# A fused two-layer backbone: three of five adaptive rounds summed on VectorE, and the zero stores moved behind the 22nd group

## The reference

```
s_lat = jax.nn.silu(c)
s_ctx = jax.nn.silu(c_ctx)
for layer in range(DEPTH):
    mod_l = jnp.split((s_lat @ ada_w[layer] + ada_b[layer])[:, None, :], 6, axis=-1)
    mod_c = jnp.split((s_ctx @ ada_w[layer] + ada_b[layer])[None, None, :], 6, axis=-1)
    hl = modulate(rmsnorm(xl, norm_g[layer, 0]), mod_l[0], mod_l[1])
    hc = modulate(rmsnorm(xc, norm_g[layer, 0]), mod_c[0], mod_c[1])
    ... mixer (layer 0: retention and a gated linear recurrence; layer 1: attention), then
    ... a mixture of 32 experts, top 2 of a group, for every token
return rmsnorm(xl, final_norm_g)
```

## Time and profile before

| | before |
|---|---|
| median of 3 runs | 2051.31 us (2050.94 to 2054.58) |
| the profiled execution | 2053.72 us |
| its span, first to last instruction | 2052.0 us |
| mean granted TensorE clock in it | 0.914 |
| TensorE matmul busy in the span | 1720.2 us (84%) |
| VectorE busy | 679.7 us (33%) |
| ScalarE busy | 439.6 us (21%) |
| GpSimd busy | 272.4 us (13%) |
| groups of this stage on TensorE | from 40.30 us to 350.67 us |

### The profile page before, as it was taken

One profiled execution on the slowest core, in us unless ns is written; L12 is line 12 of the kernel. 1 busy time (PEld: TensorE's weight loads), 2 busy tenths in 40 slices (PEclk: granted clock), 3 DMA queues, 4 the chain that ended last, 5 costly groups with the idle time before them and its releaser, 6 DMA issues. The chain is left out here.

```text
span 2052.0 us, 26634 instructions
## 1 busy us (share of the span) xinstructions
PE 1720.2 (84%) x9184; PEld 875.8 (43%) x9185; DVE 679.7 (33%) x1211; ACT 439.6 (21%) x842; POOL 272.4 (13%) x393
## 2 busy tenths in 40 slices
PE   5999999899899789996629999999977799765560
PEld 2443344645445334443317455555543344332230
DVE  3404765743312111111134337774332111111114
ACT  3104453211011101111124135553101101111012
POOL 1002440311101000001022220000111001000001
PEclk9999999998899899998868999999979899877775
DMA  9887744443599999999962002002379999999984
GB/s 371 272 296 235 268 160 144 168 157 140 216 358 406 418 411 417 416 417 410 425 244 90 39 7 87 1 1 96 142 278 399 411 416 414 412 415 421 420 359 149
DMA packets 99608, 559.64 MB, mean 273 GB/s; under 512 B 17188, under 2 KB 37376, under 8 KB 59976
## 3 DMA queue, kind: packets, MB, share of 16 engines
q1 hardware_dynamic: 86288, 521.34, 64.0%
q0 software_dynamic: 7744, 20.98, 3.0%
q10 hardware_dynamic: 5496, 16.26, 2.1%
HBM read 522.88 MB, written 40.91 MB: 275 GB/s over the span
## 5 line engine op out<-in xcount | busy, mean ns | idle before, releaser
L2198 PE MATMUL exp_gps<-moew_wg,all_hT 128*32 128x256 f32 x832 | 128.4, 477 | 102.9 <-DMA moew_wu<-in_moe_w_up 95.3
L577 PE MATMUL abp_ps<-home_pieces,all_hT 128*128 128x512 f32 x384 | 169.8, 597 | 0.6 <-PE abp_ps L581 0.3
L2204 PE MATMUL exp_gps<-moew_wg,all_hT 128*64 128x512 f32 (+1 forms) x272 | 137.8, 642 | 28.7 <-DMA moew_wu<-in_moe_w_up 24.3
L2353 DVE TENSOR_TENSOR all_hT<-all_hT,exp_ups 64x512 f32<-64x512 f32 (+1 forms) x30 | 20.7, 690 | 369.3 <-ACT all_hT L2289 369.3
L2205 PE MATMUL exp_ups<-moew_wu,all_hT 128*64 128x512 f32 (+1 forms) x272 | 136.6, 638 | 0.0
L2198 PE MATMUL exp_ups<-moew_wu,all_hT 128*32 128x256 f32 x832 | 128.3, 477 | 0.0
L2204 PE MATMUL exp_gps<-home_pieces,all_hT 128*128 128x512 f32 (+1 forms) x208 | 108.8, 635 | 22.2 <-DMA home_pieces<-in_moe_w_up 20.9
L2198 PEld LDWEIGHTS exp_gps<-moew_wg,all_hT 128*32 128x32 f32 x832 | 56.8, 136 | 160.4 <-issue 142.0
L577 PEld LDWEIGHTS abp_ps<-home_pieces,all_hT 128*128 128x128 f32 x384 | 71.4, 190 | 99.1 <-issue 97.5
L2351 DVE TENSOR_TENSOR all_hT<-all_hT,exp_ups 64x256 f32<-64x256 f32 x34 | 14.4, 425 | 283.6 <-ACT all_hT L2287 283.6
L2205 PE MATMUL exp_ups<-home_pieces,all_hT 128*128 128x512 f32 (+1 forms) x208 | 107.8, 630 | 0.0
(11 more groups left out here) (457 smaller groups left out, 2986.1 us busy)
## 6 DMA issues: line engine op xcount, KB each, us to landing
moew_wg<-in_moe_w_gate SPq DMA_DIRECT2D x43, 2048.0 KB, 25.0
moew_wu<-in_moe_w_up SPq DMA_DIRECT2D x43, 2048.0 KB, 31.7
moew_wd<-in_moe_w_down SPq DMA_DIRECT2D x43, 2048.0 KB, 39.6
home_pieces<-in_moe_w_gate SPq DMA_DIRECT2D x21, 2048.0 KB
home_pieces<-in_moe_w_up SPq DMA_DIRECT2D x21, 2048.0 KB
home_pieces<-in_moe_w_down SPq DMA_DIRECT2D x21, 2048.0 KB
all_X<-in_ada_w SPq DMA_DIRECT2D x40, 1024.0 KB, 8.3
ys<-abp_zero SPq DMA_DIRECT2D x32, 448.0 KB, 8.8
```

The costliest lines, as they stand in the source:

```text
L577: last = nc.tensor.matmul(ps[i % RB][:], hT[:, kk, what * P:(what + 1) * P], w[n % S][:, kk, :], start=(kk == 0), stop=(kk == KD - 1))
L2198: last = nc.tensor.matmul(bank[lo + j * Q:lo + (j + 1) * Q, 0:HC], x[:, k, 0:Q], wt[:, k, j * HC:(j + 1) * HC], start=(k == 0), stop=(k == ...
L2204: nc.tensor.matmul(gps[0:rows, :], x[:, k, 0:rows], w.g[q][:, k, :], start=(k == 0), stop=(k == KD - 1))
L2353: nc.vector.tensor_tensor(h[at:at + rows, :], sg[at:at + rows, :], ups[at:at + rows, :], ALU.mult).then_inc(h_done, 1)
```

## The change

Rounds 2 and 3 stay on TensorE, one step behind each of groups 2 to 9 and 26 to 33, with a ring of two buffers. Rounds 1, 4 and 5 are summed by VectorE: for each chunk `ada_sum` multiplies the 128 x 2048 chunk by the column of `sT` that belongs to it and adds it into a sum of 128 x 2048 that stays spread over the partitions. Round 1 has two sums (latent and context), rounds 4 and 5 one (latent). The chunks come through four buffers of their own. When a round's eight chunks are in, TensorE adds over the partitions (`reduce`), with a stationary operand `pick` that has a column of ones, behind group 15 (8 matmuls), 18 and 21 (4 each). The order of the rounds' outputs becomes 2, 1, 4, 5, 3. All 43 zero stores stand behind group 21 in SyncE's program, three for each group's turn.

```diff
-        RING = 3
+        TURNED = (2, 3)
+        SUMMED = (1, 4, 5)
+        ORDER = (2, 1, 4, 5, 3)
...
-        ADA_AT = [2 + 7 * r + r // 4 + at for r in range(ROUNDS - 1) for at in (0, 1, 1, 2, 2, 3, 3, 4)]
+        ADA_AT = [2 + n for n in range(KD)] + [26 + n for n in range(KD)]
+        SUM_AT = [2, 3, 5, 6, 8, 9, 11, 12] + [12 + n // 2 for n in range(KD)] + [16 + n // 2 for n in range(KD)]
+        CLEAR_FROM = 22
+        REDUCE_AT = {15: 1, 18: 4, 21: 5}
+        OUT_AT = {9: 0, 16: 1, 19: 2, 23: 3, 33: 4}
...
+            sp.wait_ge(first_used, 3)
+            for n in range(SR):
+                if n < RING:
+                    ring_chunk(n)
+                sum_chunk(n)
...
+                for n in range(len(SUM_AT)):
+                    if SUM_AT[n] == i:
+                        if n == KD - SR:
+                            sp.wait_ge(ring_used, KD)
+                        sp.wait_ge(sum_used, n + 1)
+                        sum_chunk(n + SR)
+                        if n + 1 == len(SUM_AT):
+                            for m in range(RING):
+                                ring_chunk(KD + m)
+                for b in range(cleared_to, min(BLOCKS, 3 * (i + 1 - CLEAR_FROM))):
+                    clear_slots(b)
+                    cleared_to = b + 1
+                if i in OUT_AT:
+                    n = OUT_AT[i]
+                    l, cols = ada_columns(ORDER[n])
+                    sp.wait_ge(mod_done, n + 1)
+                    for st in range(2):
+                        sp.dma_start(c.mods[st, l, cols].rearrange("(j n) -> j n", n=512),
+                                     bias_rows(bias, st)).then_inc(stored, 16)
+                    sp.wait_ge(stored, 32 * (n + 1))
+                    if n + 1 < len(ORDER):
+                        load_bias(sp, ORDER[n + 1], bias, b_ready)
...
+            def reduce(r):
+                n = SUMMED.index(r)
+                pe.wait_ge(sum_used, KD * (n + 1))
+                pe.wait_ge(mod_done, ORDER.index(r))
...
+                for st, total in enumerate(sums[r]):
+                    for j in range(4):
+                        last = nc.tensor.matmul(aps[32 * j:32 * j + 32, :], pick[:, st, :], total[:, j * 512:(j + 1) * 512],
+                                                start=(st == 0), stop=(st + 1 == len(sums[r])))
...
+            def ada_sum(n):
+                r, kk = SUMMED[n // KD], n % KD
+                buf = sum_ring[n >= KD][n % SR]
+                dve.wait_ge(sum_ready[n % SR], 16 * (n // SR + 1))
...
+                if n == 2 * KD:
+                    dve.wait_ge(reduced, 1)
+                for st, total in enumerate(sums[r]):
+                    s_col = sT[:, kk, st:st + 1]
+                    if kk == 0:
+                        last = V.tensor_scalar(total, buf, s_col, None, ALU.mult)
+                    else:
+                        last = V.scalar_tensor_tensor(out=total, in0=buf, scalar=s_col, in1=total, op0=ALU.mult, op1=ALU.add)
...
-                if ct == LT - 1:
-                    ada_out(1)
...
+                ada_sum(LT + ct)
+                if ct == 2:
+                    ada_out(2)
+            for n in range(KD, 2 * KD):
+                ada_sum(n)
+            ada_out(1)
+            for n in range(2 * KD, 3 * KD):
+                ada_sum(n)
+            ada_out(4)
+            out_before = {2: 5, 7: 3}
```

More of the change, by code:

```diff
@@ L360, in ab_project @@
         ada_first = [flat_rows[:, i * AC:(i + 1) * AC] for i in range(6)] + [flat_y[:, 0:AC], flat_x[:, 0:AC]]
-        ada_ring = [c.X[:, 2 * i:2 * i + 2, :].rearrange("p t n -> p (t n)") for i in range(RING)]
+        x_parts = [c.X[:, 2 * i:2 * i + 2, :].rearrange("p t n -> p (t n)") for i in range(3)]
+        row_parts = [flat_rows[:, i * AC:(i + 1) * AC] for i in range(6)]
+        ada_ring = x_parts[0:2]
+        RING = len(ada_ring)
+        sum_ring = [row_parts[0:3] + x_parts[2:], x_parts[0:2] + [row_parts[2]] + x_parts[2:]]
+        SR = len(sum_ring[0])
+        sums = {1: row_parts[3:5], 4: row_parts[5:6], 5: row_parts[3:4]}
         tables = small_tables(nc, a, k, s, lam, carve(flat_x[:, AC:]),
@@ L385, in ab_project @@
         ring_ready = [s.sem(f"ring_ready{i}") for i in range(RING)]
+        sum_ready = [s.sem(f"sum_ready{i}") for i in range(SR)]
+        sum_used, reduced, picked = s.sem("sum_used"), s.sem("reduced"), s.sem("picked")
         (w_free, mm, ev_act, cleared, z_set, z_stored, p_ready, gw_ready, x_ready, gates, sig,
@@ L459, in _ @@
             sp.wait_ge(scaled, NT)
-            for n in range(RING):
-                ring_chunk(n)
+            sp.wait_ge(first_used, 3)
[3 more added lines that the diff above has]
+                sum_chunk(n)
             sp.dma_start(cs[:], a["ret_cs"]).then_inc(cs_ready, 16)
@@ L501, in _ @@
             nc.gpsimd.memset(bias[:], 0.0).then_inc(zeroed, 1)
+            nc.gpsimd.memset(pick[:], 0.0).then_inc(zeroed, 1)
+            pool.wait_ge(zeroed, 4)
+            for st in range(2):
+                nc.gpsimd.memset(pick[:, st, st:st + 1], 1.0).then_inc(picked, 1)
             tables.early(pool)
@@ L615, in _ @@
             act.dma_start(laid[NB:NL, :], a["lru_lambda"][0].rearrange("d (c p) -> (d c) p", p=P)).then_inc(p_ready, 16)
-            act.wait_ge(zeroed, 3)
+            act.wait_ge(zeroed, 4)
             load_bias(act, 0, bias0, b0_ready)
-            load_bias(act, 1, bias, b_ready)
+            load_bias(act, ORDER[0], bias, b_ready)
             act.wait_ge(c_ready, 32)
@@ L735, in _, with between @@
                                     ALU.mult, ALU.add).then_inc(aff_dve, 1)
-            tables.vector(dve)
+            def between(part):
+                for n in range(2 * part, 2 * part + 2):
+                    ada_sum(n)
+            tables.vector(dve, between)
             V.tensor_scalar(n4[:], k.sp[:, 2 * RH:], LRU_C / 2, None, ALU.mult).then_inc(n4_done, 1)
@@ L822, in gpsimd, with vector @@
                                     pattern=[[0, RH], [sign, P]], channel_multiplier=-sign).then_inc(masked, 1)
-    def vector(dve):
+    def vector(dve, between):
         link = Chain(dve, chain)
@@ L834, in vector @@
         dve.wait_ge(e_in, 1)
+        between(0)
         dve.wait_ge(e_out, 1)
@@ L852, in vector @@
         V.tensor_scalar(k.dec[:], lg3, float(P), None, ALU.mult).then_inc(dcols, 1)
+        between(1)
         dve.wait_ge(masked, 2)
```

42 lines of the change are left out of this document (23 added, 19 removed).

## The result

| | before | after |
|---|---|---|
| median of 4 runs each | 2051.12 us (2050.81 to 2054.58) | 2030.01 us (2027.47 to 2031.82) |
| after over before | | 0.988, 95% interval 0.9861 to 0.9900 |
| the profiled execution, its span | 2053.72, 2052.0 us | 2031.82, 2029.8 us |
| mean granted TensorE clock | 0.914 | 0.910 |
| first matmul of retention | 352.52 us | 329.75 us |

The change makes the kernel 1.2% faster, 21 to 29 us by the interval; the two medians of the table differ by 21.1 us. In the two profiles the whole of it lies in the first stage, as expected: retention begins 22.8 us earlier, and the rest of the span is as long as before.

The account below looks back on a forecast made before the run. TensorE was taken to bound the first stage and weight transfers the expert stages. Terms -17.9 - 3.7 + 1.5 + 1.7 = -18.4 from the 2051.31 us median gave 2032.9 us, own range 2031 to 2037, wider range 2027 to 2044.

Parts of the forecast that it names:

- The sums: VectorE's chunk sums in the first stage: 2.35 us each, 70.9 us in all, against idle stretches of 101.8 us.
- The store to mods: SyncE's second small store waits behind queued chunks until near 155 us, so chunks 22 and 23 land at 163 and 165.
- Rival 3: VectorE's sums cost double, 4.7 us instead of 2.35; the kernel is 28.5 us slower, 2079.8 us; chance 0.07.
- The zero stores: Behind group 21 they cost TensorE nothing; a rival had them end the stage, 2038 us, chance 0.05.
- Rival 1: All hidden: the store passes quickly, VectorE is done by 169, 20 to 21.6 us gained, 2030.5 us; chance 0.13.
- VectorE late: Unit 0 starts at 170.5 us, so TensorE waits for ScalarE's copy before group 24 and at later copies: 1.7 us.
- new waits for chunks: TensorE waits for round 2's third chunk and the chunk behind weight block 2: 1.5 us, between 0 and 4.
- threshold of 169.2: Unit 0 may start up to 169.2 us without cost to TensorE; each later microsecond costs one.
- steps and reductions: On TensorE's chain 37.75 us of steps go and 19.85 us of steps and reductions come: 17.9 us gained.
- waits for chunks of before: TensorE's two waits for chunks go, as the zero stores leave that stretch: 3.7 us gained, bounded by 0 and 3.7.

Follow-up runs that it names:

- e4: The changed kernel with the second store to mods moved from group 16's to group 17's turn in SyncE's program; 2029.44 us, ratio 0.9864 to before.
- e5: The changed kernel with two extra operations of the sums' shape on VectorE ahead of unit 0; ratio 0.9907 to before.
- e6: The changed kernel with four extra operations of the sums' shape on VectorE ahead of unit 0; ratio 0.9931 to before.
- e3: The changed kernel with the zero stores put back to the groups at which they stood before; 2039.38 us, ratio 0.9925 to before.
- e7: The changed kernel with both the two extra VectorE operations and the second store to mods one group later; ratio 0.9894 to before.
- e9: The kernel before, unchanged, run against itself; ratio 1.0004, retention begins at 355.27 us.
- e11: The kernel before, unchanged, profiled once more in a single run; no ratio, retention begins at 355.01 us.
- e1: The changed kernel itself, run again beside the kernel before; 2029.29 against 2056.01 us, ratio 0.9867.
- e12: The kernel before with the eight zero stores that go with round 2's steps issued at the end of the stage; ratio 0.9950 to before.
- e10: The changed kernel without round 3's 32 matmuls and without GpSimd's rotations of the row groups; 2020.44 us, ratio 0.9822 to before.
- e2: The kernel before with only the zero stores moved behind group 21, three for each group's turn; 2051.82 us, ratio 0.9983 to before.
- e8: The changed kernel without the 32 matmuls of round 3, its chunks still loaded; 2029.79 us, ratio 0.9871 to before.

## Why the prediction was right in its mechanism and wrong in its size

**What held.** The stage is bound by TensorE and its gain comes through whole. The steps: 37.75 us forecast to go, 16.0 + 3.85 to come, and a step, a double and a single reduction measure 1.0, 1.86 and 1.0. The sums: 2.35 us forecast from two rows of other widths, 2.35 measured. The store to mods: held until about 155 by forecast, until 156.93 by the trace, with chunks 22 and 23 behind it; e4 showed the cause. Rival 3, sums at double price, was off: the 28 sums with an addition took 67.4 us, 2.41 each. VectorE's forms of 0 to 330 us, busy, mean ns, idle before:

```profile
L753 DVE SCALAR_TENSOR_TENSOR home_pieces<-all_X,abp_sT,home_pieces 128x2048 f32<-128x2048 f32 x14 | 34.9, 2507 | 1.8 <-DMA all_X<-in_ada_w 0.7
L753 DVE SCALAR_TENSOR_TENSOR home_pieces<-home_pieces,abp_sT 128x2048 f32<-128x2048 f32 x14 | 32.5, 2349 | 10.6 <-DMA home_pieces<-in_ada_w 10.3
```

Only two of them cost much more, 3.37 and 3.15, beside GpSimd. The zero stores did not end the stage: the last seven are issued from 306.90 to 315, the stage ends at 327.87.

Rival 1 has the nearest number, 2030.5, but only half of its condition held: VectorE was done by 169 (168.68), while the store did not pass quickly (10.8 us).

**What was mis-sized.** Two terms of the sum, *VectorE late* (+1.7) and *new waits for chunks* (+1.5), measured 0. Without them the sum is -21.6, beside the 21.1 us by which the medians differ. The difference between the two first profiles, -22.8 against the sum of -18.4, goes to these terms:

| term | forecast | measured | how |
|---|---|---|---|
| steps and reductions | -17.9 | -17.9 | timeline |
| waits for chunks of before | -3.7 | -4.1 | 69.27 to 71.80 and 122.36 to 127.60, less two doubles of 1.85 |
| new waits for chunks | +1.5 | 0 | none in the waits view |
| VectorE late | +1.7 | 0 | group 24 without a wait |
| first groups, start | 0 | +0.7 | 16.32 instead of 15.47, begun 0.15 earlier; mean granted clock from 40 to 60 us 0.88 instead of 0.92 |
| hand-overs between unlike matmuls | 0 | -1.5 | what remains |

The step that failed first is *VectorE late*. My own working gave an end of the sums at 168.3, under the threshold of 169.2, and I then took 170.5 by leaning towards the upper bound. The end was 168.68. The threshold was right, and the start nearly at its edge: 0.3 us to spare at the copy of group 21, and e5 shows 6.1 us of stage lost for 6.1 of start. A value that the working gives should not be rounded towards the danger without a row that speaks for it. The same holds for the *new waits for chunks*, where the dates of landing of 67 to 70 against 68.4 gave nearly even odds and I booked 1.5 us.

The threshold's mechanism held, with one wait left out: I named only group 24 behind unit 1's square root. Group 22 behind unit 0's has its own threshold. In the profile of after ScalarE starts the two copies behind that square root at 180.09 and ends the first by about 180.7, 3.7 us ahead of group 22 at 184.33, so by my estimate the wait there begins with a start of unit 0 at about 172.4. With starts of 174.82 (e5), 180.69 (e6) and 183.67 (e3) it is there, with 170.56 (e7) it isn't.

The *hand-overs* I had priced within a step. The remainder fits two neighbours of like shape: two groups without a step between them take 14.00 us where one takes 7.13, so the second begins after 6.87, and not 7.07 as a step does behind a group. Six channel groups in one run, 103.80 to 135.33 with 0.30 idle, take 31.5 us where three pairs of before, at 7.07 + 3.65 each, would be 32.2. But of the 39 places where one group follows another, 16 now have nothing between them and 12 had nothing before; four more at 0.2 us are 0.8 of the 1.5. The other 0.7 stay unassigned, and the attribution is by subtraction and wasn't tested alone.

**What was missed.** The *waits for chunks* of before were priced by one profile. In e9 and e11 the waits and what they bring sum to more: 72.24 - 69.05 - 1.85 = 1.3 and 128.75 - 122.87 - 1.85 = 4.0, and 1.5 for the slow group, 6.9 us where I took 3.7. Against e9 the stage of e1 is 355.27 - 329.18 = 26.1 us shorter, which is close to the 26.7 measured in e1's session, though the rest of the span differs between the two profiles by 3 us the other way (1695.4 and 1698.4). The sentence that failed is "the stretch with the wait of 3.2 us kept a granted clock of 1.00": it was true of that execution and is not a property of the kernel. e12 shows the price with the wait removed. Whether the first session's kernel before, 2051 instead of 2056 us, had fewer such falls can't be said from one profile.

**Left open.** The rest of the span behind the stage lay between 1692.7 and 1702.7 us over all profiles, with either kernel's code there, and no run is about it. Executions with a higher mean clock tend to be shorter (in one session the kernel before had a span of 2049.4 us at 0.919 and of 2059.2 at 0.909), but not strictly so. The 5 us by which e12's time is better than its stage shows belong there or to executions that weren't profiled.

## What to carry to other kernels

Take the ready time that the working gives, compare it with the threshold, and put the doubt into the range, not into the value. Price a wait of TensorE's from several executions, as its length and the slower matmuls behind it. Before moving more work off TensorE, check the loop beside it: here leaving out the last 8 us of steps alone gave 1.1 us of stage, and 7.7 together with leaving out GpSimd's rotations (e1 to e10).

## What the runs showed of the hardware

- The granted clock falls to 0.50 behind some waits of TensorE's and not behind others of like length. It fell behind 2.29 us (e5), 2.59 (e3), 3.27 (e2), 3.31 (e11), 3.69 (e9), 4.41 (e3), 4.49 (e8) and 8.95 (e6), and stayed at 1.00 behind 2.83 (e7) and 3.18 (the first profile of before). Behind a wait with a fall two row groups took 15.67 to 16.87 us instead of 14.00, or one wide group 7.79 to 8.83 instead of 7.13. What decides it no run here shows; the kernel before did it in two of three profiles.
- A multiply and add of 128 x 2048 on VectorE takes 2.35 us alone, and 2.92 (e1) to 3.83 (e3) beside GpSimd; a multiply of 768 columns 0.96 and 1.90. The Trainium skill says that GpSimd and VectorE share their SBUF interfaces, with contention for operations with two SBUF inputs ("GPSIMD Engine Reference", "Key points"); both of these have two, and the trace agrees.
- A store of a few KB, issued behind fresh chunks on the one queue, took 10.8 us until SyncE went on (profile of after, 146.10 to 156.93), and 2.3 with a quiet queue (profile of before, 212.01 to 214.30).
